# Opening of a float32 transformer stack on one core: x by features from the host, loads by quarters, two token blocks per weight quarter

## What is computed

```python
def swiglu(x, w_in, w_out):
    gate, up = jnp.split(x @ w_in, 2, axis=-1)
    return (jax.nn.silu(gate) * up) @ w_out

h = x
h = layer_norm(DN_ALPHA * h + 0.5 * swiglu(h, ffn_w_in[0, 0], ffn_w_out[0, 0]), ln_g[0, 0], ln_b[0, 0])
```

## Time and profile before

| | |
|---|---|
| median of 3 runs | 1522.62 us (1522.59 to 1522.76) |
| profiled execution | 1522.67 us, span 1520.9 us |
| TensorE busy | 1512.6 us, 8164 matmul passes |
| VectorE busy | 968.4 us |
| ScalarE busy | 755.7 us |
| GpSimd busy | 131.2 us |
| DMA | 283.71 MB, mean 187 GB/s |

### The profile page before, as it was taken

One profiled execution on the slowest core, in us unless ns is written; L12 is line 12 of the kernel. 1 busy time (PEld: TensorE's weight loads), 2 busy tenths in 40 slices (PEclk: granted clock), 3 DMA queues, 4 the chain that ended last, 5 costly groups with the idle time before them and its releaser, 6 DMA issues.

```text
span 1520.9 us, 20479 instructions
## 1 busy us (share of the span) xinstructions
PE 1512.6 (99%) x8164; PEld 1300.4 (86%) x8164; DVE 968.4 (64%) x981; ACT 755.7 (50%) x724; POOL 131.2 (9%) x141
## 2 busy tenths in 40 slices
PE   9999999999999999999999999999999999999998
PEld 8888889888888888888888888888898888888886
DVE  5556576765567556577667655557686556785555
ACT  5454465554545454454434445455536566354442
POOL 1000020100002000024021200002002200020000
PEclk9999999999999999999999999999999999999999
DMA  8554564355545654555544455556443444455551
GB/s 311 196 192 172 213 221 166 133 218 205 192 169 188 226 191 175 211 213 203 175 163 166 171 225 186 183 203 224 168 166 141 160 144 167 166 213 202 189 187 67
DMA packets 42264, 283.71 MB, mean 187 GB/s; under 512 B 5088, under 2 KB 5536, under 8 KB 9552
## 3 DMA queue, kind: packets, MB, share of 16 engines
q1 hardware_dynamic: 38016, 270.55, 48.6%
q0 software_dynamic: 2368, 8.59, 1.7%
q10 hardware_dynamic: 1808, 3.55, 0.6%
HBM read 281.55 MB, written 1.05 MB: 186 GB/s over the span
## 4 chain that ended last, share of the span: by engine, by line
PE 99%; DMA 0%; ACT 0%; DVE 0%; SPq 0%; DVEq 0%; POOLq 0%; issue 0%; POOL 0%; ACTq 0%
PE psum L1687 21%; PE psum L1582 17%; PE psum L1585 16%; PE psum L1586 16%; PE psum L1691 11%; PE psum L1714 5%; PE psum L1721 3%; PE psum L1627 2%; PE psum L1614 2%; PE psum L1620 2%; PE psum L1594 1%; PE psum L2113 0%; DMA weights_raw<-in_weights 0%; PE psum L2076 0%; PE psum L2134 0%; PE psum L1967 0%
## 5 line engine op out<-in xcount | busy, mean ns | idle before, releaser
L914 DVE TENSOR_TENSOR weights_lo<-weights_raw,weights_hi 128x2048 fp32r<-128x2048 f32 x247 | 569.8, 2318 | 318.5 <-ACT weights_hi L434 317.2
L434 ACT ACTIVATE weights_hi<-weights_raw 128x2048 fp32r<-128x2048 f32 (+1 forms) x254 | 479.5, 1890 | 297.5 <-PE psum L1586 140.7
L1687 PE MATMUL psum<-operand,weights_hi 128*128 128x512 f32 x1376 | 327.6, 390 | 0.0
L1687 PEld LDWEIGHTS psum<-operand,weights_hi 128*128 128x128 f32 x1376 | 255.3, 188 | 51.1
L1582 PE MATMUL psum<-weights_hi,hidden_hi 128*128 128x512 f32 x480 | 187.7, 391 | 0.0
L1585 PE MATMUL psum<-weights_lo,hidden_hi 128*128 128x512 f32 x480 | 187.6, 391 | 0.0
L1586 PE MATMUL psum<-weights_hi,hidden_lo 128*128 128x512 f32 x480 | 186.8, 389 | 0.0
L1691 PEld LDWEIGHTS psum<-operand,weights_lo 128*128 128x128 f32 x1376 | 176.4, 191 | 6.7
L1691 PE MATMUL psum<-operand,weights_lo 128*128 128x256 f32 x1376 | 178.5, 283 | 0.0
L1582 PE MATMUL psum<-weights_hi,operand 128*128 128x512 f32 x384 | 151.6, 395 | 0.0
L1585 PE MATMUL psum<-weights_lo,operand 128*128 128x512 f32 x384 | 149.8, 390 | 0.0
(11 more groups left out here) (297 smaller groups left out, 1828.8 us busy)
## 6 DMA issues: line engine op xcount, KB each, us to landing
weights_raw<-in_weights SPq DMA_DIRECT2D x254, 1024.0 KB, 4.8
ln_rows<-in_ln_rows POOLq DMA_DIRECT2D x16, 512.0 KB, 6.8
weights_raw<-in_weights SPq DMA_DIRECT2D x4, 512.0 KB, 6.6
normalised<-in_x SPq DMA_DIRECT2D x2, 512.0 KB, 6.1
ret_constants<-in_ret_constants ACTq DMA_DIRECT2D x1, 1024.0 KB, 7.3
out<-normalised SPq DMA_DIRECT2D x4, 256.0 KB, 2.0
gla_w_low<-in_gla_w_low ACTq DMA_DIRECT2D x1, 512.0 KB, 5.5
att_w_small<-in_att_w_small ACTq DMA_DIRECT2D x1, 512.0 KB, 5.7
```

Of the source, the lines that this page charges most:

```text
L434: nc.scalar.activation(w_hi[:, s, whole], raw[:, s, whole], ACT.Copy).then_inc(hi_split, 1)
L914: nc.vector.tensor_tensor(w_lo[:, s, :], raw[:, s, :], w_hi[:, s, :].bitcast(F32), ALU.subtract).then_inc(lo_split, 1)
L1687: mm(banks[b // 2][:, b % 2, :], w_hi[:, slot, cols], x_both[:, c, :, :].rearrange("p a t -> p (a t)"), start=c == 0, stop=False, skip_gro ...
```

## The change

The host gives x a second time, by features (`x_turned`: four pieces of two chunks, each 128 x 512, for all 256 tokens), and lays weight tile 0 out as four quarters of its own. SP loads chunk pairs and quarters of tile 0 in turn, tile 1 by halves between the last chunk pairs, then the identity. The turned x lies in the third ring buffer, so tile 2's load waits until all four rests of x are made; x itself (for the residual) is loaded behind tile 2, ahead of the ring loop. TensorE warms 10 times, then does for each quarter both token blocks: 6 products a quarter, with no transposes of x; it frees tile 0 in the middle. ScalarE and VectorE alternate one x piece and two weight quarters. GpSimd's wait for the operand is gone.

```diff
+        x_raw = raw[:, 2, :].rearrange("p (c t) -> p c t", c=KC)
...
-        turns, at = {"x": 0}, KC // 2
+        turns, at = {}, 0
...
         @block.sync
         def _(sp):
-            sp.dma_start(xn[:, 0, :], io["x"][0]).then_inc(x_loaded[0], 16)
-            for n in range(2):
-                for j in range(2):
-                    cols = slice(j * D, (j + 1) * D)
-                    sp.dma_start(raw[:, n, cols], io["weights"][n][:, cols]).then_inc(weight_loaded[n] if j else half_loaded[n], 16)
-            sp.dma_start(xn[:, 1, :], io["x"][1]).then_inc(x_loaded[1], 16)
+            first_tile = io["weights"][0].rearrange("p n -> (p n)").rearrange("(k p n) -> k p n", k=4, p=P)
+
+            def load_chunks(g):
+                sp.dma_start(raw[:, 2, g * NCOL:(g + 1) * NCOL], io["x_turned"][g]).then_inc(chunks_loaded[g], 16)
+
+            def load_quarter(k):
+                sp.dma_start(raw[:, 0, k * NCOL:(k + 1) * NCOL], first_tile[k]).then_inc(quarter_loaded[k] if k < 3 else weight_loaded[0], 16)
+
+            load_chunks(0)
+            load_quarter(0)
+            load_quarter(1)
+            load_chunks(1)
+            load_quarter(2)
+            load_quarter(3)
+            load_chunks(2)
+            sp.dma_start(raw[:, 1, 0:D], io["weights"][1][:, 0:D]).then_inc(half_loaded, 16)
+            load_chunks(3)
+            sp.dma_start(raw[:, 1, D:], io["weights"][1][:, D:]).then_inc(weight_loaded[1], 16)
+            sp.dma_start(ident, io["constants"][:, 0, :]).then_inc(ident_loaded, 16)
+            sp.wait_ge(x_lo_done, KC // 2)
             sp.dma_start(raw[:, 2, :], io["weights"][2]).then_inc(weight_loaded[2], 16)
+            for tb in range(TB):
+                sp.dma_start(xn[:, tb, :], io["x"][tb]).then_inc(x_loaded[tb], 16)
...
             pool.wait_ge(x_loaded[0], 16)
             pool.wait_ge(x_loaded[1], 16)
-            pool.wait_ge(operand_ready, KC // 2)
...
-            act.dma_start(ident, io["constants"][:, 0, :]).then_inc(ident_loaded, 16)
-            rows_hi("x", 0, block_acc(0), (0,))
-            quarters_hi(0)
-            rows_hi("x", 0, block_acc(0), (1,))
-            quarters_hi(1)
-            rows_hi("x", 1, block_acc(1))
+            def quarter_hi_first(n, k):
+
+                cols = slice(k * NCOL, (k + 1) * NCOL)
+                act.wait_ge((half_loaded if k < 2 else weight_loaded[1]) if n else quarter_loaded[k] if k < 3 else weight_loaded[0], 16)
+                nc.scalar.activation(w_hi[:, n, cols], raw[:, n, cols], ACT.Copy).then_inc(first_hi if k < 3 else hi_split, 1)
+
+            def x_hi_first(g):
+
+                act.wait_ge(chunks_loaded[g], 16)
+                nc.scalar.activation(x_hi[:, 2 * g:2 * g + 2, :], x_raw[:, 2 * g:2 * g + 2, :], ACT.Copy).then_inc(x_hi_done, 1)
+
+            for n in range(2):
+                x_hi_first(2 * n)
+                quarter_hi_first(n, 0)
+                quarter_hi_first(n, 1)
+                x_hi_first(2 * n + 1)
+                quarter_hi_first(n, 2)
+                quarter_hi_first(n, 3)
             split_hi(2)
...
+            def x_lo_first(g):
+
+                dve.wait_ge(x_hi_done, g + 1)
+                part = lambda t: t[:, 2 * g:2 * g + 2, :]
+                nc.vector.tensor_tensor(part(x_lo), part(x_raw), part(x_hi).bitcast(F32), ALU.subtract).then_inc(x_lo_done, 1)
...
+            def opening_unit(out):
+
+                def products(n, k, x, w, start=False, stop=False):
+                    for tb in range(TB):
+                        last = mm(out[:, tb, :], x[:, 4 * n + k, tb * P:(tb + 1) * P], w[:, n, k * NCOL:(k + 1) * NCOL],
+                                  start=start, stop=stop, skip_group_check=True)
+                    return last
...
                 for n in range(2):
                     for k in range(4):
                         hi_by_hi(n, k)
+                        lo_by_hi(n, k)
                         if k:
+                            hi_by_lo(n, k - 1)
+                    hi_by_lo(n, 3).then_inc(weights_used, 1)
 
             pe.wait_ge(warm_ready, 1)
-            warm(8)
+            warm(10)
+            opening_unit(pairs[0])
             pe.wait_ge(ident_loaded, 16)
-            turn_x1 = turn_rows("x", xn, 1, block_acc(1), x_loaded[1], lambda b: 16)
-            opening_unit(pairs[0], turn_rows("x", xn, 0, block_acc(0), x_loaded[0], lambda b: 16), turn_x1)
-            first_unit(N_FFN0, pairs[0], "x", turn_x1, blocks=(1,))
             ffn(N_FFN0, 0)
...
     tiles = ffn(0, 0)
+    tiles[0] = tiles[0].reshape(P, 4, NCOL).transpose(1, 0, 2).reshape(P, TILE)
...
         "x": a["x"][0].reshape(TB, P, D),
+        "x_turned": a["x"][0].T.reshape(KC // 2, 2, P, TOK).transpose(0, 2, 1, 3).reshape(KC // 2, P, 2 * TOK),
```

More of the change, by code:

```diff
@@ L201, in build @@
         warm_ready = sem("warm_ready")
-        half_loaded = [sem(f"half_loaded{n}") for n in range(2)]
+        chunks_loaded = [sem(f"chunks_loaded{g}") for g in range(KC // 2)]
+        quarter_loaded, half_loaded = [sem(f"quarter_loaded{k}") for k in range(3)], sem("half_loaded")
+        x_hi_done, x_lo_done = sem("x_hi_done"), sem("x_lo_done")
         first_hi, first_lo = sem("first_hi"), sem("first_lo")
@@ L1058, in ffn, with quarter_lo_first @@
                 last_step(10, n0 + 28)
[L1060 to L1066, removed]
-            nc.vector.memset(squares[:, 0:P], 1.0).then_inc(warm_ready, 1)
[L1069 to L1073, removed]
+            def quarter_lo_first(n, k):
+                cols = slice(k * NCOL, (k + 1) * NCOL)
+                dve.wait_ge(first_hi if k < 3 else hi_split, 3 * n + k + 1 if k < 3 else n + 1)
+                nc.vector.tensor_tensor(w_lo[:, n, cols], raw[:, n, cols], w_hi[:, n, cols].bitcast(F32),
+                                        ALU.subtract).then_inc(first_lo if k < 3 else lo_split, 1)
+            def x_lo_first(g):
+                dve.wait_ge(x_hi_done, g + 1)
+                part = lambda t: t[:, 2 * g:2 * g + 2, :]
+                nc.vector.tensor_tensor(part(x_lo), part(x_raw), part(x_hi).bitcast(F32), ALU.subtract).then_inc(x_lo_done, 1)
+            nc.vector.memset(squares[:, 0:P], 1.0).then_inc(warm_ready, 1)
+            for n in range(2):
+                x_lo_first(2 * n)
+                quarter_lo_first(n, 0)
+                quarter_lo_first(n, 1)
+                x_lo_first(2 * n + 1)
+                quarter_lo_first(n, 2)
+                quarter_lo_first(n, 3)
             split_lo(2)
@@ L1600, in turn_normed, with first_unit @@
                 return turn_rows(f"ln{ln}", xn, tb, block_acc(tb), xn_ready, lambda b: 4 * (ln - 1) + 2 * tb + b + 1)
-            def first_unit(n, out, what, turn_second, blocks=range(TB)):
-                for tb in blocks:
+            def first_unit(n, out, what, turn_second):
+                for tb in range(TB):
                     t = slice(tb * P, (tb + 1) * P)
@@ L1846, in hi_by_hi @@
                 def hi_by_hi(n, k):
-                    if k == 0:
-                        pe.wait_ge(turned_hi, turns["x"] + n + 1)
+                    pe.wait_ge(x_hi_done, 2 * n + k // 2 + 1)
                     pe.wait_ge(first_hi if k < 3 else hi_split, 3 * n + k + 1 if k < 3 else n + 1)
-                    by_hi(n, k, x_hi, (n, k) == (0, 0))
+                    products(n, k, x_hi, w_hi, start=(n, k) == (0, 0))
                 def lo_by_hi(n, k):
-                    if k == 0:
-                        pe.wait_ge(operand_ready, turns["x"] + n + 1)
@@ L1855, in lo_by_hi @@
-                    by_hi(n, k, x_lo, False)
+                    pe.wait_ge(x_lo_done, 2 * n + k // 2 + 1)
+                    products(n, k, x_lo, w_hi)
                 def hi_by_lo(n, k):
                     pe.wait_ge(first_lo if k < 3 else lo_split, 3 * n + k + 1 if k < 3 else n + 1)
[L1859 to L1863, removed]
@@ L1864, in opening_unit @@
-                warm(5)
+                    return products(n, k, x_hi, w_lo, stop=(n, k) == (1, 3))
                 for n in range(2):
                     for k in range(4):
-                        if (n, k) == (1, 3):
-                            turn_second[0]()
                         hi_by_hi(n, k)
+                        lo_by_hi(n, k)
                         if k:
[L1871 to L1876, removed]
+                            hi_by_lo(n, k - 1)
```

## The result

The changed kernel takes 1525.7 us in the median of 20 runs (1524.66 to 1527.3), the kernel before 1522.6 (1522.48 to 1522.9): a ratio of 1.0022, 95% interval 1.0016 to 1.0028. It is slower by 3.1 us, at the very edge of what I called distinguishable, and its runs spread over 2.6 us where those of before spread over 0.4. The profiled execution took 1525.60 us, with a span of 1523.8.

What follows compares the result with a forecast made beforehand. TensorE's one string of matmuls bounds the kernel. The opening gains 3.0 us, but late tiles 2 and 3 move the hidden transposes from 25.30 to 27.0: 1522.67 + 1.7 = 1524.4 us, range 1522.2 to 1526.3.

Steps and rivals of the forecast that it cites:

- the two stalls: TensorE stands 2.35 us before line 1687 for tile 2, then 2.45 us before the hidden transposes for hidden.
- TensorE's own gain: The opening's products start near 5.4 instead of 7.39 and end at 16.65, 3.0 us ahead of 19.64.
- Tile 2 by itself: Tile 2's load, alone on SP's emptied queue behind the fourth x rest, lands at 17.1, about 4.7 us after issue.
- Tile 3 4.95 behind it: Tile 3's load, on SP's queue behind tile 2, x 0 and x 1, lands at 22.05.
- From tile 3's landing to the transposes: Tile 3 is rounded from 22.05 to 24.0, its rest made by 26.3, hidden by 27.0, when the hidden transposes start.
- the fourth x rest: VectorE makes the last rest of turned x from 11.5 to 12.2; tile 2's load waits for it.
- the landing of tile 1's first half: In the opening's load queue, this half tile lands at 9.55, read by bytes off the earlier trace's curve.
- The prediction named the price of a quarter-megabyte load as its open figure: Opening loads with 2 KB rows: half of 1.25 us taken; half of 2.05 as upper bound, mark 28.3, +3.0.
- Rival 3: Small loads in the opening are slow, carrying the x rest to about 13.5: 1525.7 us; chance 0.13.
- The 1539 us: By the skill's rule of some 2 us per load, the fourth x piece lands some 14 us later.
- Rival 1: Tile 2 or 3 come early enough that earlier products count: 1519.7 us, or 1522.0 with only the second stall gone; chance 0.12.
- Rival 2: TensorE's clock falls in the second stall, before the hidden transposes, costing 1.9 us: 1526.3 us; chance 0.12.

Runs made afterwards that it cites:

- e3: The changed kernel with turned x in the residual's buffer (no wait ahead of tile 2) and x 0 and x 1 loaded behind tile 4; 1520.52 us.
- e7: The changed kernel with x 0 and x 1 behind tile 4, wait kept, plus 12 warm-up matmuls in the stall ahead of line 1717; 1523.34 us.
- e1: The changed kernel with x 0 and x 1 loaded behind tile 4 instead of ahead of tile 3, wait ahead of tile 2 kept; 1524.99 us.
- e4: The changed kernel with x and tile 0 loaded by halves of 512 KB (4 KB rows) instead of quarters; 1527.04 us.
- e5: The changed kernel with 12 more warm-up matmuls between the opening's products and line 1717, in the first stall; 1526.13 us.
- e2: The changed kernel with turned x in the residual's buffer, so no wait ahead of tile 2; x 0 and x 1 stay ahead of tile 3; 1522.64 us.
- e8: e3 with x and tile 0 loaded by halves of 512 KB instead of quarters; 1523.06 us.

## Why the prediction was right, and where it was off

The forecast was 1524.4 us, in a range of 1522.2 to 1526.3, with no change over 0.2% as the likeliest; measured were 1525.7, ratio 1.0022. The direction and the two stalls are right, the size is 1.3 us short, and the class at the bound fell to the other side, which had 0.14.

- TensorE's own gain, 3.0 us in the opening: the loads of the products ended at 17.13, so line 1717 could have started 2.5 us earlier than 19.64. Right but for 0.5 us: the loads waited 0.22, 0.20 and 0.52 us for the third and fourth quarter of tile 0 and the first of tile 1, where the prediction had almost nothing. As said, the end doesn't see it. e3 shows it freed: line 1722 at 17.71.
- Tile 2 by itself takes 4.75 us from issue: measured 4.85 (13.66 to 18.51). Tile 3 4.95 behind it: measured 4.90. From tile 3's landing to the transposes 4.95: measured 4.89. These terms held to 0.1 us each, and the two predicted stalls are there, 3.4 and 0.78 us on the weight loads for 2.35 and 2.45. That the second is short comes from the half clock, which filled it from TensorE's side.
- The term that was mis-sized is the fourth x rest: 12.2 predicted, 13.63 measured. The step that failed in it is the landing of tile 1's first half, 9.55 by the curve of the earlier trace rows and 11.06 in the profile (10.34 to 11.06 in the five with this queue); the 1.4 us went through to the end one for one. The prediction named the price of a quarter-megabyte load as its open figure, and put it at the low bound. That isn't shown to be the fault: in e7 all seven quarters ahead of tile 1 landed at the predicted times or before, but for 0.2 us, and the half was as late. The loss is at 8 to 10 us, with 269 GB/s for 414, and its reason is open.
- Rival 3 (small loads are slow) had 0.13 and gave the measured time, 1525.7, but its mechanism isn't confirmed, so that its number was met may be luck. By its own price of 1.025 us a quarter, tile 1's first half lands at 3.9 + 6 x 1.025 + 1.25 = 11.3, the x rest at 13.9 and not at 13.5. The 1539 us that the prediction worked out from the Trainium skill's page "DMA: Bandwidth & Descriptors" are refuted. The 2 us per load stand there in the section "Anatomy of one DMA", for loads that GpSimd issues, not in "Bandwidth".
- Rival 1 (the loads are not the end) is refuted by e1 to e3. Its figure for the whole gain, 1519.7, is near what e3 reaches, 1520.5.
- Rival 2 (the clock): it did fall, but in the first stall, where its 1.3 us were covered, as the prediction said of the first. Behind the second stall it falls in e4 and e5, and costs 1.6 us there where I took 1.9. The Trainium skill's section "HAM oscillation" was read too widely: the waits that it describes are longer than the 2.45 us predicted. The 2.14 us wait of e2's profiled run left the clock at full pace, and some of e2's other runs are 2 us slower than it; none of those was profiled.
- TensorE's warm-up and clock before the wait don't matter to the end, and nothing behind 27 us takes the offset back: both right (1497.3 us from the transposes on, in every kernel whose clock stayed up there).
- The waits of the weight loads over the whole run, called a few us, add up to 12 in the view of the earlier trace rows. Nothing hangs on it.

## What to carry to other kernels

When a load is put behind a wait on an in-order queue, or another load ahead of it, follow that queue to its next user and add up landings: here a gain of 2.5 us at the front of the opening was turned into a loss of 3.1 by one borrowed buffer and two loads that nobody needed for over 100 us. A mean rate over a window is no price of a load: look at when each load landed, and at how far runs of the same queue differ. Lend a buffer whose next user is far away, and queue what isn't urgent behind what is. Choose a single instruction late in the disturbed stretch as the mark; if the time from there on is constant, all the rest is arithmetic.

## What the runs showed of the hardware

A pause of TensorE of 3.4 us on its weight loads let the granted clock fall to half in the changed kernel and in e1. Pauses of 2.22 us (e4), 2.17 (e5) and 2.11 (e4, for its first quarter) did so too, each only after the pause had ended; pauses of 2.14 (e2) and 2.12 (e3, in the opening) didn't. So among those near 2.1 us the length alone doesn't tell. Where the fall wasn't covered it cost 1.4 to 1.6 us in the profiles.

Loads of 256 KB with 2 KB rows, queued back to back, moved 308 to 372 GB/s from 6 to 8 us; halves with 4 KB rows moved 363 and 373 in e8 and e4, and 418 in the kernel before. From 8 to 10 us the kernels with quarters throughout moved 269 to 335 GB/s, those with halves 406 to 414. The same queue landed the same load anywhere within 0.7 us over five profiled runs. The prediction gave a fall of the clock in so short a wait 0.12, and had no loss from 8 to 10 us.
